# A two-block network on one core: the order of work between the mixer, the experts and the next layer

## What is computed

```python
x = x + gt_a * (merged @ w_o)                 # end of the mixer
h = rms_norm(x, g_ffn) * (1 + sc_f) + sh_f
top_val, top_idx = top_k(h @ w_router + b_router, 4)   # 4 of 32 experts
gates = softmax(top_val)
for e in range(32):                           # for the rows that chose e
    u = h @ w1[e] + b1[e]                     # 1024 x 2048
    glu, lin = min(u[:, ::2], 7), clip(u[:, 1::2], -7, 7)
    y += gate * ((glu * sigmoid(1.702 * glu) * (lin + 1)) @ w2[e] + b2[e])   # w2: 1024 x 1024
x = rms_norm(x + gt_f * y, g_final)           # then the two layers of the second block
```

## Time and profile before

| | |
|---|---|
| median of 3 runs | 1906.1 us (1905.62 to 1906.78) |
| profiled execution | 1905.34 us, span 1903.2 us |
| TensorE busy | 1819.9 us (96%) |
| VectorE, ScalarE busy | 787.7 us (41%), 571.7 us (30%) |
| DMA | 592.39 MB, mean 311 GB/s |

### The profile page before, as it was taken

One profiled execution on the slowest core, in us unless ns is written; L12 is line 12 of the kernel. 1 busy time (PEld: TensorE's weight loads), 2 busy tenths in 40 slices (PEclk: granted clock), 3 DMA queues, 4 the chain that ended last, 5 costly groups with the idle time before them and its releaser, 6 DMA issues. The chain is left out here.

```text
span 1903.2 us, 24278 instructions
## 1 busy us (share of the span) xinstructions
PE 1819.9 (96%) x9780; PEld 1164.3 (61%) x9780; DVE 787.7 (41%) x1158; ACT 571.7 (30%) x911; POOL 17.0 (1%) x33
## 2 busy tenths in 40 slices
PE   7999999999999999989999999999999999999998
PEld 6799888843333333333333333337888888978886
DVE  5867655411121121120211211216676655666665
ACT  4444554410011010010100100105555544645552
POOL 1000001000000000000000000000000000000000
PEclk9999999999999999999999999999999999999999
DMA  9976756599999999999999999999356556336552
GB/s 342 321 249 231 242 195 195 219 421 428 429 432 430 430 431 430 430 430 429 430 431 430 431 430 430 430 430 323 132 178 199 178 176 214 118 111 199 193 172 100
DMA packets 155402, 592.39 MB, mean 311 GB/s; under 512 B 6703, under 2 KB 85743, under 8 KB 128832
## 3 DMA queue, kind: packets, MB, share of 16 engines
q1 hardware_dynamic: 152816, 582.90, 77.6%
q0 software_dynamic: 2512, 8.45, 1.3%
HBM read 590.26 MB, written 1.07 MB: 311 GB/s over the span
## 5 line engine op out<-in xcount | busy, mean ns | idle before, releaser
L1698 PE MATMUL psum<-shared,expert_arena 128*64 128x512 f32 x1536 | 341.7, 597 | 18.8 <-DMA shared<-in_w_mlp_dram 18.8
L1549 DVE TENSOR_SCALAR expert_arena<-psum 128x512 f32<-128x512 f32 x32 | 22.1, 691 | 583.4 <-PE psum L1698 583.4
L1698 PEld LDWEIGHTS psum<-shared,expert_arena 128*64 128x64 f32 x1536 | 105.9, 137 | 238.3 <-issue 201.8
L422 PE MATMUL psum<-layer_x_parts,layer_w_hi 128*128 128x512 f32 x704 | 240.5, 396 | 0.4 <-DVE layer_x_parts L2212 0.4
L1455 ACT ACTIVATE expert_arena<-expert_arena 128x512 f32<-128x512 f32 x32 | 20.1, 629 | 562.1 <-DVE expert_arena L1549 562.1
L421 PE MATMUL psum<-layer_x_parts,layer_w_lo 128*128 128x256 f32 x616 | 171.8, 279 | 0.0
L352 DVE TENSOR_TENSOR mixer_w_lo<-mixer_ring,mixer_w_hi 128x1024 fp32r<-128x1024 f32 x96 | 116.3, 1223 | 95.9 <-ACT mixer_w_hi L347 95.7
L352 DVE TENSOR_TENSOR layer_w_lo<-slots_ahead,layer_w_hi 128x1024 fp32r<-128x1024 f32 x96 | 116.8, 1223 | 82.7 <-ACT layer_w_hi L347 82.7
L347 ACT CAST mixer_w_hi<-mixer_ring 128x1024 fp32r<-128x1024 f32 x96 | 100.0, 1048 | 158.9 <-PE psum L390 92.5
L422 PEld LDWEIGHTS psum<-layer_x_parts,layer_w_hi 128*128 128x128 f32 x704 | 125.8, 188 | 24.6 <-DVE layer_x_parts L2212 0.8
L388 PE MATMUL psum<-layer_w_hi,layer_x_parts 128*128 128x512 f32 (+1 forms) x384 | 139.1, 362 | 0.4 <-DVE layer_x_parts L2212 0.4
(11 more groups left out here) (316 smaller groups left out, 2679.2 us busy)
## 6 DMA issues: line engine op xcount, KB each, us to landing
shared<-in_w_mlp_dram SPq DMA_DIRECT2D x98, 2048.0 KB, 22.0
expert_ring<-in_w_mlp_dram SPq DMA_DIRECT2D x64, 2048.0 KB, 25.2
mixer_ring<-in_w_in_dram SPq DMA_DIRECT2D x38, 1024.0 KB, 5.8
slots_ahead<-in_w_mlp_dram SPq DMA_DIRECT2D x15, 2048.0 KB, 25.7
mixer_ring<-in_w_ada_dram SPq DMA_DIRECT2D x22, 1024.0 KB, 5.5
slots_ahead<-in_w_ffn_in_dram SPq DMA_DIRECT2D x21, 1024.0 KB, 4.9
memory_kv<-in_w_mlp_dram SPq DMA_DIRECT2D x15, 1024.0 KB, 24.7
kept<-in_w_mlp_dram SPq DMA_DIRECT2D x15, 1024.0 KB, 26.7
```

What stands on the lines that cost most here:

```text
L422: last = self.nc.tensor.matmul(out, hi, both[:, k].rearrange("p h s -> p (h s)"), start=k == 0, stop=k == KC - 1)
L1549: nc.vector.tensor_scalar(glu, both[:, :, 0], LIMIT, None, ALU.min).then_inc(glu_ready, 1)
L1698: last = nc.tensor.matmul(U[CAP * h:CAP * h + CAP, N * n:N * n + N], xg[:, k, j, :], expert_slot(M, k // 2)[:, at:at + N], start=False, st ...
```

## The change

The mixer's order at its end becomes `to0`, `to1` (the second one `apart`), `mT00`, `mT01`, `gcol`, `fcol`, `yg`, `mT10`, `mT11`, `brow`, `wo0`, `wo1` (both `apart`). The transposes of tile 0 wait for three merges, tile 0's `wo` for `mT01`, tile 1's for `mT11`. Fillers ahead of `yg`, `mT00` and `wo0t0` go. The emptying of `wo` goes through a new place `moved`, and VectorE raises the biases after `wo1t0`.

The sync queue issues the table, expert 1's first down slot and half of its second after `mT11`, as the mixer's ring places have been split (`raw_split`); then expert 0's up slot 3; after the last product expert 0's down slots; after `lg1` and `bias_ready` the last half slot.

The transposes of x wait for the quarter of x that they read; ScalarE empties tile 0's, VectorE tile 1's; the filler between them and the router goes. VectorE makes `chosen` tile by tile. The second gather of the first pair has the bank of `hT01`, waits for no `xg_ready`, and has no filler. In layer 0 all four `gain` operations stand ahead of `xT00`, and the filler ahead of `vn0t0` goes.

```diff
-    def natural(self, pe, jobs, outs, xh, xl, ready=None, part=slice(None), opened=0, only=None):
+    def natural(self, pe, jobs, outs, xh, xl, ready=None, part=slice(None), opened=0, only=None, second_tile=None):
...
+            if second_tile is not None and tiles == (T - 1,) and u == units[shared]:
+                second_tile()
...
     for half in range(2):
-        jobs.pair(f"to{half}", "dve", jobs.rows(A["w_att_o"][0], N * half))
-    jobs.add("gcol", "act")
-    jobs.add("fcol", "dve")
-    jobs.add("yg", "act")
+        jobs.pair(f"to{half}", "dve", jobs.rows(A["w_att_o"][0], N * half), apart=half == 1, ahead=2)
     for t in range(T):
         for half in range(2):
             jobs.add(f"mT{t}{half}", "dve", high=True)
+        if t == 0:
+            jobs.add("gcol", "act")
+            jobs.add("fcol", "dve")
+            jobs.add("yg", "act")
     jobs.add("brow", "dve")
     for half in range(2):
-        jobs.pair(f"wo{half}", "dve", jobs.rows(A["w_o"][0], N * half))
+        jobs.pair(f"wo{half}", "dve", jobs.rows(A["w_o"][0], N * half), apart=True, ahead=3)
...
-                    nc.vector.tensor_tensor(sig[:, t, cols], b, rows_mod[:, 0, cols], ALU.mult).then_inc(freed_by_dve, 1)
+                    moved = M["aside"]["moved"]
+                    if half:
+                        dve.wait_ge(x_ready, t + 1)
+                    nc.vector.tensor_tensor(moved[:, t, :], b, rows_mod[:, 0, cols], ALU.mult).then_inc(freed_by_dve, 1)
...
+                    if name == "wo1t0":
+                        M["aside"]["low_bias"](dve)
...
-            short = {"pT70": 1, "ao7": 1, "to0t0": 1, "yg": 2, "mT00": 4, "wo0t0": 1}
+            short = {"pT70": 1, "ao7": 1, "to0t0": 1}
...
-                        pe.wait_ge(merged_ready, 2 * T)
+                        pe.wait_ge(merged_ready, 2 * T if t else 2 * T - 1)
...
-                        wait_freed(pe, "mT11")
+                        wait_freed(pe, "mT01")
+                        second_tile = lambda: wait_freed(pe, "mT11")
...
-            jobs.add(f"hT{t}{half}", "act" if half else "dve")
+            jobs.add(f"hT{t}{half}", "dve" if t else "act")
...
+            def raw_free(n):
+                sp.wait_ge(mixed["lo_ready"], max(mixed["raw_split"][0:n]))
+
+            def first_slots_early():
+
+                sp.wait_ge(mixed["full"], mixed["merged"])
+                sp.dma_start(M["later"][:, :], A["table_later"]).then_inc(row_here, 16)
+                down_load(1, 1, 0, True, False)
+                raw_free(1)
+                second_odd(1, 0)
+                raw_free(3)
+                for k in range(AHEAD, UP):
+                    up_load(sp, M, A, 0, k)
+                sp.wait_ge(mixed["full"], mixed["products"])
+                for k in range(DOWN):
+                    down_load(0, 0, k, False, False)
+                sp.wait_ge(full, jobs.full("lg1"))
+                sp.wait_ge(bias_ready, 1)
+                second_odd(1, 1)
...
-            act.wait_ge(mixed["full"], mixed["products"])
+            act.wait_ge(mixed["full"], mixed["small_jobs"])
+            act.wait_ge(mixed["biases_here"], 16 * 8)
+            nc.scalar.copy(bias[:, :], bias_raw).then_inc(high_ready, 1)
             for t in range(T):
                 act.wait_ge(mixed["x_ready"], T + t + 1)
...
+                for half in range(2 if t == 0 else 0):
+                    act.wait_ge(full, jobs.full(f"hT{t}{half}"))
+                    nc.scalar.copy(actT[:, 4 * half:4 * half + 4, P * t:P * t + P], bank[jobs.by_name[f"hT{t}{half}"].bank].rearrange("p (k s) -> p k s", k=4)).then_inc(freed_by_act, 1)
...
-
-            step(nc.vector.tensor_copy(first, index[:, :, :]))
...
+                step(nc.vector.tensor_copy(first[:, t, :], index[:, t, :]))
+                step(nc.vector.tensor_tensor(hit[:, t], experts_row, first[:, t, 0:4].unsqueeze(2).to_broadcast([P, 4, E]), ALU.is_equal))
+                nc.vector.tensor_reduce(chosen[:, t, :], hit[:, t].rearrange("p j e -> p e j"), AX.X, ALU.add).then_inc(chosen_ready, 1)
...
-            pe.wait_ge(mixed["freed_by_dve"], mixed["counts"]["dve"])
+            pe.wait_ge(mixed["freed_by_dve"], mixed["counts"]["dve"] - 1)
             for t in range(T):
-                pe.wait_ge(mixed["x_ready"], T + t + 1)
                 for half in range(2):
+                    pe.wait_ge(mixed["x_ready"], T + t + 1 if half else t + 1)
...
-            keep_busy(nc, M, bank[BG], 4)
...
-                gather(p0, 1, busy=0 if later else 2)
+                gather(p0, 1, not later)
...
-                    for part in range(3):
+                    for part in range(2 * T):
                         dve.wait_ge(summed["sum_done"], part + 1)
                         gain(part % T, part // T)
-                if name == "xT01" and i == 0:
-                    dve.wait_ge(summed["sum_done"], 2 * T)
-                    gain(T - 1, 1)
...
-            short = {"qm": 5, "ao7": 1, "yT10": 5, "fg0": 3} if i else {"xT00": 1, "vn0t0": 3, "pT0:0": 2}
+            short = {"qm": 5, "ao7": 1, "yT10": 5, "fg0": 3} if i else {"xT00": 1, "pT0:0": 2}
```

More of the change, by code:

```diff
@@ L1224, in on_tensor, with raw_split @@
             keep_busy(nc, M, spare, 4)
+        def raw_split(k):
+            return max(job_units[-1] + 1 for q, (_, _, job_units) in enumerate(jobs.slots) if job_units and stream.aside_of(q) is None and stream.turn(q) % RING_MIX == k)
         return Stage(on_sync, on_gpsimd, on_scalar, on_vector, on_tensor, x_ready=x_ready, biases_here=biases_here, full=full, products=jobs.full("wo1t1"),
+                     merged=jobs.full("mT11"), small_jobs=jobs.full("brow"), lo_ready=stream.lo_ready, raw_split=[raw_split(k) for k in range(RING_MIX)], last_bank=jobs.by_name["wo1t1"].bank,
                      freed_by_act=freed_by_act, freed_by_dve=freed_by_dve, counts=dict(jobs.counts), fcol=jobs.by_name["fcol"].freed, brow=jobs.by_name["brow"].freed)
@@ L1300, in experts @@
     PAIRS = E // 2
-    jobs = Jobs(range(BANKS))
+    jobs = Jobs([n for n in range(BANKS - 1) if n != mixed["last_bank"]])
     for t in range(T):
         for half in range(2):
-            jobs.add(f"hT{t}{half}", "act" if half else "dve")
+            jobs.add(f"hT{t}{half}", "dve" if t else "act")
     for t in range(T):
@@ L1331, in wait_freed, with gathered_bank, low_bias @@
             eng.wait_ge(freed[job.by], job.freed)
+        def gathered_bank(part, first_pair):
+            return bank[jobs.by_name["hT01"].bank if part and first_pair else BG]
+        def low_bias(dve):
+            dve.wait_ge(row_here, 16)
+            dve.wait_ge(high_ready, 1)
+            nc.vector.scalar_tensor_tensor(bias[:, :], bias[:, :].bitcast(FP32), const(M, "low_rows"), bias_raw, ALU.mult, ALU.add).then_inc(bias_ready, 1)
         def second_flag(eng):
@@ L1487, in on_vector @@
             step = Chain(dve, step_sem)
+            for half in range(2):
+                dve.wait_ge(full, jobs.full(f"hT1{half}"))
+                nc.vector.tensor_copy(actT[:, 4 * half:4 * half + 4, P:2 * P], bank[jobs.by_name[f"hT1{half}"].bank].rearrange("p (k s) -> p k s", k=4)).then_inc(freed_by_dve, 1)
             dve.wait_ge(squares_ready, T)
@@ L1492, in on_vector @@
             dve.wait_ge(scale_ready, 1)
-            for t in range(T):
-                dve.wait_ge(full, jobs.full(f"hT{t}0"))
-                nc.vector.tensor_copy(actT[:, 0:4, P * t:P * t + P], bank[jobs.by_name[f"hT{t}0"].bank].rearrange("p (k s) -> p k s", k=4)).then_inc(freed_by_dve, 1)
             dve.wait_ge(row_here, 16)
+            experts_row = numbers[:, 0:1, 0:E].to_broadcast([P, 4, E])
             for t in range(T):
@@ L1669, in gather @@
             def gather(pairs, part, first_of_all=False, busy=0):
-                keep_busy(nc, M, bank[0], busy)
+                keep_busy(nc, M, bank[BG], busy)
                 pe.wait_ge(picked, pairs + 1)
@@ L1681, in gather @@
                         at = 2 * P * (2 * part + k // 2) + k % 2
-                        last = nc.tensor.matmul(bank[BG][:, P * k:P * k + P], hn[:, t, at:at + 2 * P - 1:2], pick[:, t].rearrange("p j s -> p (j s)"), start=t == 0, stop=t == T - 1)
+                        last = nc.tensor.matmul(gathered_bank(part, first_of_all)[:, P * k:P * k + P], hn[:, t, at:at + 2 * P - 1:2], pick[:, t].rearrange("p j s -> p (j s)"), start=t == 0, stop=t == T - 1)
                 last.then_inc(gathered, 1)
```

63 lines of the change are left out of this document (30 added, 33 removed).

## The result

The changed kernel takes 1895.99 us (median of 6 runs, 1894.99 to 1896.98); the kernel before took 1906.44 beside it (6 runs, 1905.41 to 1907.51). The ratio is 0.9941, 95% interval 0.993 to 0.9951: 10.4 us less, by the interval 9.3 to 13.3. The prediction said 1896.9, with 1894.5 to 1899 for its likeliest case. The profiled execution took 1896.98 us, span 1895.2.

The account below looks back on a forecast made before the run. The expert weight stream sets the stage's later pace, its start tied to TensorE. Stream 7.3 plus layer 0 1.9 make 9.2 us off 1905.34: 1896.1 profiled, 1896.9 on the median; range 1892.5 to 1901.5.

Parts of the forecast that it names:

- its likeliest case: The forecast itself: a median of 1896.9 us, own range 1894.5 to 1899, chance 0.55.
- What bounds the stage: Expert stage: the weight stream sets the later pace, but its start is tied to TensorE freeing slots in experts 0 and 1.
- The seam: From the mixer's end to expert 0's first product: four savings on TensorE start that product 6.9 us earlier, at 372.9.
- `wo` earlier: Mixer's end: without fillers, and with transposes waiting for three merges, TensorE reaches `wo` 2.9 us earlier; bounds 0 and 3.4.
- filler ahead of the router: Between the transposes of x and the router: dropping the filler saves 1.73 us.
- router by tile: Router: tile 0's operations fall into the wait for tile 1's logits, saving 0.4 us; bounds 0 and 0.6.
- second gather: First pair of experts: the second gather no longer waits for ScalarE and loses its fillers, saving 1.85 us.
- The dry gap and the restart: Sync queue after the early loads: dry at about 371, restarted at 376.6; restarting costs 1.9 us, another 0.5 at expert 3.
- the stream's gain of 7.3 us: Expert stage: the weight stream runs 7.3 us earlier by expert 3; bounds 5.4 and 8.7.
- Layer 0: Layer 0's beginning: all four quarters of x written first, so the first product starts 1.9 us earlier; bounds 0 and 1.9.
- The single fall: Rival: with fewer fillers, TensorE's clock falls once, for 4 us in the seam, giving 1898.9 us; chance 0.07.
- one of the prediction's own signs of being wrong: Signs listed against the forecast: a clock under 1.00 in the seam, DMA share of 1 through 378, `wo` waiting for a split.

Follow-up runs that it names:

- busy_pairs: Changed kernel with two filler products more at the head of each of the 15 pairs of experts; 1898.06 us, ratio 0.9955.
- after_again: The changed kernel, unaltered, run and profiled a second time; 1897.18 us, ratio 0.9947.
- old_layer0: Changed kernel with layer 0's beginning as before (fourth quarter of x after two split transposes, filler ahead of the first product); 1897.85 us, ratio 0.995.
- loads_alone: Kernel before with only the early loads and the buffers they take; TensorE's order, fillers, router, gathers and layer 0 as before; 1906.03 us, ratio 0.9991.
- moved_filler: Changed kernel with the mixer's last four fillers moved from ahead of the transposes of x to ahead of the router's products; 1896.33 us, ratio 0.9941.
- no_end_filler: Changed kernel without the mixer's last four filler products; 1895.83 us, ratio 0.9935.
- before_again: The kernel before, unchanged, run and profiled a second time; 1906.23 us, ratio 0.9994.
- old_order: Changed kernel with the old order of small jobs and the fillers at the mixer's end, `wo` still tile by tile; 1898.88 us, ratio 0.9957.

## Why the prediction was right, point by point

**What bounds the stage: right.** Through all twelve profiles the last scatter comes 890.4 to 891.3 us after expert 2's first issue, while that issue itself moves by 8.0 us (80.74 to 88.78). And expert 2's issue comes 25.44 or 25.45 us after expert 0's first product, in every kernel but busy_pairs, which puts 0.87 us between them. That is the tie that was read from one window of 397 GB/s and the issue 1.8 us ahead of it. One reading was stronger than its rows: the queue of before did not run dry at 407, for expert 2's loads were already in it, and the windows of 2 us show 426 GB/s at 404 to 406 and then 377, 360 and 369, a dip and no pause. What shows the tie is the constant 25.44 us.

**The seam: right, by its parts.** Without the clock's fall:

| term | predicted | measured | from |
|---|---|---|---|
| `wo` earlier | 2.9 | 2.5 | 334.90 - 316.07 = 18.83, before 337.80 - 316.45 = 21.35 |
| filler ahead of the router | 1.73 | 1.73 | last product to router 3.63, before 5.36 |
| router by tile | 0.4 | 0.41 | router to first gather 7.98 (after_again), before 8.39 |
| second gather | 1.85 | 1.92 | first gather to first product 4.43, before 6.35 |
| sum | 6.9 | 6.6 | 63.33 - 56.74 = 6.59 |

`wo` came at the forecast moment because this execution was early by 0.4 us; the small jobs took 5.66 us (329.24 to 334.90) where 5.38 were counted. The splits were in time: VectorE did both at 335.66, in 2.36 us, and `wo` waited for neither.

**The dry gap and the restart: right.** The queue was dry from about 371.1 (the window 370 to 372 moved 242 GB/s, that behind it 8); 371 was predicted. From the issue at 377.84 to 384 are 6.16 us; the windows moved 147 x 2 + 393 x 4 = 1866 KB, 4.34 us at 430 GB/s. The restart cost 1.8 us, against 1.9 in the sum. The Trainium skill (DMA: Bandwidth & Descriptors, section "Latency and other measured facts") has 0.6 us to the first byte; the trace shows 147 GB/s in the two microseconds from 378 and 393 in the four behind them, so the ramp belongs to the price, and the measured 1.8 us decides. The queue ran low once more at expert 2's issue (385 to 400 moved 406 GB/s, 400 to 407 moved 346: 2.2 us short of 430), and 0.6 us went at expert 3's (414 GB/s in 420 to 435), near the 1.9 and 0.5 of the sum. Of the stream's gain of 7.3 us, the 0.4 beyond TensorE's start came out at 0.2 (890.68 against 890.84, after_again), 0.4 in old_layer0.

**One detail wrong, without cost.** The down slot in `memory_kv` was to go out with the table at about 333. It waited for the ring's first place to be split, until 345.75, and up slot 3 went at 349.58. TensorE waited for neither.

**Layer 0: right.** 2.08 us measured, 1.9 predicted.

**The clock: the rival came true in part.** The single fall had 0.07. It occurs in some executions, takes 1.33 us from the seam instead of 2, and with it one of the prediction's own signs of being wrong (a clock under 1.00 in the seam) was seen, while the rest of the account held. It leaves the profiled execution of after at 979.50 us from first load to layer 0's first product, against 986.94 before: 7.4 us. Without it (after_again, 978.11) the gain of this stretch is 8.8; the sum was 9.2. The ground given against it was wrong: it was weighed by the longest pause, and TensorE had no pause at all in the stretch in which the clock fell.

**The median: near, and in part by luck.** The medians differ by 10.4 us, the two first profiles by 8.4. The profile of before (1905.34) lies 1.1 us under the median of its runs, that of after (1896.98) 1.0 over the median of its own and highest of the six; these two are the missing 2 us. Of the 8.4 us, 7.4 are in the traced stretch, 0.4 lie ahead of the first load, 0.2 behind the stretch, and 0.4 outside the span: time less span is 2.1 us in before and 1.7 to 1.9 in every changed version, loads_alone too, and no run shows why. What makes other executions longer is not on record. Falls of the clock by 1.3 us in the seam and 1.6 in layer 0 (last section) would be of that size, but this is not shown. No term of the sum answers for these 2 us: the median came out 0.9 under 1896.9 although the stretch gained 7.4 to 8.8 us where 9.2 were summed.

## What to carry to other kernels

A load that starts early is worth what the next tie allows: find the first slot that the consumer must free, and count the gain from there. Here 5.85 MB loaded into an empty queue were worth 0.4 us alone and 0.9 behind an earlier TensorE, and 6.6 us off the consumer's start were worth 6.6. A bound by transfers in the middle of a stage does not make the consumer's work at its beginning free; with a ring of fixed size the stream's place was set there once, and what TensorE did after that was free up to its waits (busy_pairs).

## What was not expected of the hardware

TensorE's clock fell to the lower level (1.2 GHz) in a stretch without any pause: in the changed kernel's first profile, TensorE ran transposes from 358.49 and 32-column products from 360.39, busy throughout, and then the windows from 364 to 368 were granted 0.52 and 0.63; at 370 it was at 1.00 again. The same instructions in the same order kept 1.00 in the second profile. What decides between them no run here shows.

The clock falls elsewhere too, with the old seam as well as the new. In layer 0 TensorE waits 1.78 us for ScalarE in all twelve profiles. In four of them (loads_alone, moved_filler, no_end_filler, busy_pairs) the clock then falls to 0.50, in eight it stays at 1.00. The products behind the wait and a window of 2 us behind it, first in moved_filler, then in after_again:

```profile
1344.84 3.13 PE L2436 MATMUL psum<-memory_kv,shared 64*128 64x256 f32 x16 [1.78 <-ACT shared L2144]
1346.00:1348.00 2.00, 2.00 (x11) 1.35 (x8) 1.88 (x5) 0.96 (x3) 0.00 (x0) 0.50 0.72 187
...
1345.21 2.09 PE L2437 MATMUL psum<-memory_kv,shared 64*128 64x256 f32 x16 [1.78 <-ACT shared L2145]
1346.00:1348.00 2.00, 2.00 (x20) 1.64 (x16) 1.58 (x4) 1.03 (x4) 0.00 (x0) 1.00 0.52 129
```

From layer 0's first product to the end of the span it is 601.2 to 601.5 us in the four, 599.5 to 599.9 in the eight: the fall costs some 1.6 us. The prediction held against the clock's fall that a pause of 1.71 us had passed at 1.00; one trace was too few for that. In five profiles (before_again, loads_alone, after, old_order, no_end_filler) the clock is near 0.50 from 20 to 40 us as well, and no cost shows: the first load of expert weights is issued at 316.07 to 317.21 us in these, at 316.01 to 316.81 in the others.
